# Gate products in whole units: double steps in the latent and differential attention of a hybrid layer

## Chip, cores and metric

The kernel runs on one core of one Trainium2 chip. The metric is the device time of one execution in microseconds. Three runs of the kernel before gave 2636.66, 2638.37 and 2639.43 us; their median is 2638.37.

## The reference

The whole computation is two blocks on 512 tokens of width 2048, all in fp32. The first block is two hybrid layers. A layer normalises x, multiplies by w_in (5952 columns), and feeds three attentions, of which two matter here; their outputs are gated with silu, multiplied by w_out, normalised and added to x. The second block (pooling, a diagonal state-space model, an embedding gate) is not touched.

```
C, latent ("MLA"), 4 heads:    p = softmax(causal((q_nope.k_nope + q_rope.k_rope) * 192**-0.5));  o = p @ v
A, differential, 4 heads:      p0, p1 = softmax of two 64-wide score matrices;  o = (p0 - lam * p1) @ v
B, sliding window, 16 heads:   softmax over a band of 128 keys with a sink logit
y = concat(A, B, C) * silu(concat(a_g, b_g, c_g));   out = y @ w_out
```

Both C and A run over blocks of 128 queries with a causal mask: query block qb of a head sees (qb + 1) * 128 keys. The gate columns a_g, b_g, c_g are ordinary products h @ w_in.

## The kernel before

**Products.** Every wide product takes three TensorE products in the fp32r format, each 512 columns (the tokens) long: high part by high part, high by low, low by high (lines 1923 to 1925, `product`). Weights come in units: 4 k-tiles by 256 output columns. SP loads a unit into one of four slots (ring), ScalarE casts its high part (L613, two halves), GpSimd subtracts to get the low part (L597, two halves), and TensorE then runs 2 banks x 4 k-tiles x 3 = 24 products on it. `unit` waits for wlo_done before it starts; each bank's last product raises mm_done. A ScalarE cast into a slot waits for mm_done of the unit four before. Four units with the same output columns make one round of two PSUM banks of gemm_ps, which VectorE then copies out (bank_taken).

**Attention.** An attention is 16 items, one for each head h and query block qb; item m has h = m // 4 and qb = m % 4. Each engine goes through steps m = 0 to 19 (LAST) with its own part of several items:

- TensorE (`attention`, L2132): score_step(m), then a half of a gate unit, tp_step(m - 2) (transposes of the probabilities, L2101), pv_step(m - 3) (probabilities times values, L2128).
- VectorE (L1266): copies of the gate round and the gate arithmetic at m = 9, 10, 18 and 19 (GATES_AT), out_step(m - 4) (copy of a finished head, only for qb = 3), max_step(m) (L1221, L1222), norm_step(m - 1) (L1239 to L1244).
- ScalarE (L718): the gate's tanh at m = 9 and 18, exp_step(m) (L673 or L680), pt_step(m - 2) (copy of the transposed probabilities, L700), then the weight casts (split_until) at steps that finish a unit.

A score in C is two fp32 matrices (L2082, L2083; each in two passes), in A six fp32r products of 64 rows (L2078, two row halves side by side), both followed by bf16 mask products (L2086; one in C, two in A).

**What they wait for.** C keeps its scores in s_ps, one bank for even and one for odd items: score_step(n) waits for the exponentials of item n - 2. In A the even items use both banks of s_ps, the odd ones banks 1 and 2 of to_ps (a_scores); score 1 of A also waits, at its own lines, for the rotations of A and of all copies out of av:

```
                    if m == 1:
                        pe.wait_ge(roped, l * ROPE_N + ROPES["B"])
                        pe.wait_ge(o_taken, 12 * l + 4)
                        pe.wait_ge(bank_taken[1], at[("av", l)][1] + 2)
```

av_take(1) on VectorE (L1454) raises that bank_taken[1]. tp_step(n) waits for norm_step(n) (normed) and, since there is one bank t_ps for all transposes of C and A, for pt_step(n - 1) (p_copied). pv_step(n) waits for p_copied of item n; pt_step(n) waits for tp_step(n) and pv_step(n - 2).

**Which half where.** HALF_AT maps a step to a half unit h (unit h // 2, bank h % 2). In C and A it is h + h // 6: steps 0 to 5, 7 to 12 and 14 to 17 have a half of 12 products, steps 6, 13, 18 and 19 none. ScalarE casts the weights four units ahead at the step of each odd half. C is interleaved with the gate columns "bg0", A with "cg", B with "ag"; behind C come the 576 products of "aqk" and the 192 of "av".

Of the kernel before, what the change touches and what calls it, by code (L numbers as in the profile page):

```python
# [188 lines left out]
def build_program(nc, x, positions, w_in, w_uq, w_ukv, w_out, p_2, w_in_2, w_pool_2, w_glu_2, w_out_2, w_ple_2,  # L189
                  w_ple_gate_2, params, ssm_params, consts, out):  # L190
    at, UNITS, ROUNDS = plan_units()
    with ExitStack() as ctx:
# [49 lines left out]
        c_at, n = {}, 0  # L242
# [141 lines left out]
            return l * ATT_ITEMS + FIRST[br] + m, m // 4, m % 4  # L384

        LAST = 16 + 4
        HALF_AT = {br: {h + h // 6 if br != "B" else h: h for h in range(16)} for br in "CAB"}
        GATES_AT = {br: {9: 0, 18: 1} if br != "B" else {8: 0, 16: 1} for br in "CAB"}
        ROPES = {"C": 0, "A": 3, "B": 11}
        ROPE_N = 20  # L390
# [214 lines left out]
        def _(act):  # L605
# [112 lines left out]
            def attention(l, br, key, g0):  # L718

                u0 = at[key][0]  # L720
                for m in range(LAST):
# [11 lines left out]
                    if m - 1 in GATES_AT[br] and g0 % GATE_ROUNDS < SPILLED:  # L733
                        gate_store(g0 + GATES_AT[br][m - 1])
                    if HALF_AT[br].get(m, 0) % 2 and (br != "B" or m != 15):
                        split_until(u0 + HALF_AT[br][m] // 2 + 1 + RING)
                    if m == 16 and br == "B":
# [1179 lines left out]
        def _(pe):  # L1917
# [56 lines left out]
            def one_pair(key, p, j, op=wide_op, banks=PAIR, order=(0, 1, 2, 3), ps=gemm_ps, tiles_of=None):  # L1974

                u0, r0 = at[key]
                unit(p * 4 + (u0 + j), j, [p + r0, p + r0] if ps is gemm_ps else None, banks, op,
                     order[j] * UK, UK, j == 0, j == 3, ps, VERS[tiles_of] + 4 * j if tiles_of else None)
# [61 lines left out]
            def score_step(l, br, m):  # L2040
                n, h, qb = item(l, br, m)
                q = slice(qb * 128, qb * 128 + 128)
                nk = (qb + 1) * 128
                if br == "B" and m:
                    pe.wait_ge(shifted, l * 16 + m)
                elif br == "C" and m:
                    if n >= 2:
                        pe.wait_ge(exped, n - 1)
                elif br == "A" and m:
                    pe.wait_ge(exped, n - 1)  # L2050
# [4 lines that stand above are left out]
                elif n:  # L2055
                    pe.wait_ge(exped, n)
                if br == "B":
                    w0 = 0 if qb else 128
                    g = h // 2
                    if qb == 0:  # L2060
                        pe.wait_ge(roped, l * ROPE_N + ROPES["B"] + 1 + 2 * (h + 1))
                    for a in range(2):
                        for s in range(2):
                            mm = pe.matmul(s_ps[:, a, s * 256 + w0:(s + 1) * 256],  # L2064
                                           tiles[64 * a:64 * a + 64, 4 + 2 * h + s, q],
                                           k_dup[64 * a:64 * a + 64, g, (qb - 1) * 128 + w0:nk],
                                           start=True, stop=True)
                    mm.then_inc(scores, 1)
                    return
                if br == "A":  # L2070
                    if qb == 0:
                        pe.wait_ge(qk_ready, 8 * l + 2 * (h + 1))
                    q_hi, k_hi = qk_high(h), qk_high(4 + h)
                    q_lo, k_lo = tiles_r[:, h], tiles_r[:, 4 + h]
                    for i, (left, right) in enumerate(((q_hi, k_hi), (q_hi, k_lo), (q_lo, k_hi))):
                        for c in range(2):
                            rows = slice(64 * c, 64 * c + 64)
                            pe.matmul(a_scores[n % 2][:, c, 0:nk], left[rows, q], right[rows, 0:nk],  # L2078
                                      start=i == 0, stop=i == 2, skip_group_check=True)
                else:  # L2080
                    c = n % 2
                    pe.matmul(s_ps[:, c, 0:nk], tiles[:, 12 + h, q], tiles[:, h, 0:nk], start=True, stop=False)  # L2082
                    pe.matmul(s_ps[:, c, 0:nk], tiles[:, 9 + h // 2, q], tiles[:, K_ROPE[h % 2], 0:nk],  # L2083
                              start=False, stop=True)
                for c in range(2) if br == "A" else (n % 2,):
                    mm = pe.matmul((a_scores[n % 2] if br == "A" else s_ps)[:, c, q], ident_b[:], mask_b[:],  # L2086
                                   start=False, stop=True, skip_group_check=True)
                mm.then_inc(scores, 1)

            def tp_step(l, br, m):  # L2090
                n, h, qb = item(l, br, m)
                b = n % 2
                pe.wait_ge(normed, n + 1)
                if n:
                    pe.wait_ge(p_copied, n)
                if br == "B" and m == 0:
                    pe.wait_ge(roped, (l + 1) * ROPE_N)
                blocks = [(0, k) for k in range(qb + 1)] if br != "B" else \
                    [(a, 2 * s + k) for a in range(2) for s in range(2) for k in range(0 if qb else 1, 2)]
                for a, k in blocks:  # L2100
                    mm = pe.transpose(t_ps[:, a, k * 128:(k + 1) * 128],  # L2101
                                      prob[n % 3][:, a * 512 + k * 128:a * 512 + (k + 1) * 128], ident)
                mm.then_inc(p_tp, 1)

            def pv_step(l, br, m):
                n, h, qb = item(l, br, m)
                b = n % 2
                q = slice(qb * 128, qb * 128 + 128)
                pe.wait_ge(p_copied, n + 1)
                if br == "B" and m == 0:  # L2110
                    pe.wait_ge(v_in, l + 1)
                if qb == 0 and br == "C" and h >= 2:
                    pe.wait_ge(o_taken, n // 4 - 1)
                elif qb == 0 and n // 4 and (br != "C" or h == 0):
                    pe.wait_ge(o_taken, n // 4)
                if br == "B":
                    g = h // 2
                    for s in range(2):
                        for a in range(2):
                            for k in range(0 if qb else 1, 2):  # L2120
                                mm = pe.matmul(o_ps[64 * a:64 * a + 64, s, q],
                                               v_b[:, qb - 1 + k, 64 * g:64 * g + 64],
                                               prob_t[:, b, (4 * a + 2 * s + k) * 128:(4 * a + 2 * s + k + 1) * 128],
                                               start=k == (0 if qb else 1), stop=k == 1)
                else:
                    v0 = 8 if br == "A" else 4
                    for k in range(qb + 1):
                        mm = pe.matmul(o_ps[:, 1 if br == "A" else h % 2, q], tiles[:, v0 + k, h * 128:(h + 1) * 128],  # L2128
                                       prob_t[:, b, k * 128:(k + 1) * 128], start=k == 0, stop=k == qb)
                mm.then_inc(pv_done, 1)  # L2130

            def attention(l, br, key):  # L2132

                for m in range(LAST):
                    if m < 16:
                        score_step(l, br, m)
                    if br == "B" and m == 8:
                        tp_step(l, br, m - 2)
                    if m in HALF_AT[br]:
                        p, j, f = HALF_AT[br][m] // 8, HALF_AT[br][m] // 2 % 4, HALF_AT[br][m] % 2  # L2140
                        one_pair(key, p, j, banks=[PAIR[0], None] if f == 0 else [None, PAIR[1]])
                    if br == "B" and 16 <= m < 19:
                        one_pair(("wo", l), 0, (m - 16) // 2, tiles_of=f"y{l}",
                                 banks=[PAIR[0], None] if m != 17 else [None, PAIR[1]])
                    if 2 <= m < 18 and (br != "B" or m != 8):
                        tp_step(l, br, m - 2)
                    if 3 <= m < 19:
                        pv_step(l, br, m - 3)
# [3 lines left out]
            for l in range(LAYERS):  # L2152
# [56 lines left out]
                    tokens_unit(u0 + 2 + n, 2 + n, sub_op, 2 * n, n == 0, n == 1)  # L2209
                pe.wait_ge(bank_taken[0], r0 + 4)  # L2210
                pe.wait_ge(roped, l * ROPE_N + 3)
                attention(l, "C", ("bg0", l))
                pairs(("aqk", l), 4)
                pe.wait_ge(p_copied, l * ATT_ITEMS + 16)
                pe.wait_ge(o_taken, 12 * l + 4)
                for n in range(8):
                    tokens_unit(at[("av", l)][0] + n, n % 4, wide_op, 2 * n, n == 0, n == 7)
                pe.wait_ge(bank_taken[0], at[("av", l)][1] + 2)
                attention(l, "A", ("cg", l))
                for j in range(4):  # L2220
                    one_pair(("bq0", l), 0, j)
                    if j == 2:
# [237 lines left out]
```

## Time and profile before

| what | value |
|---|---|
| runs | 2636.66, 2638.37, 2639.43 us |
| profiled execution, its own time | 2639.56 us |
| span of its records | 2637.7 us |
| TensorE busy | 2586.3 us, 98% of the span |
| VectorE, ScalarE, GpSimd busy | 53%, 36%, 45% |
| mean DMA rate | 106 GB/s |

The busy share of TensorE counts modelled ends: a product's record is longer than the distance to the next one, so records overlap. For what TensorE can do, take distances between starts. A line such as "x2" in a timeline merges neighbours of one kind.

### The profile page before, as it was taken

Reading aid. Unit: us, or ns where it says so; the run is one execution under the profiler, and the core shown is the slowest. Engines: PE = TensorE matmul, PEld = TensorE weight load, DVE = VectorE, ACT = ScalarE, POOL = GpSimd, SP = SyncE. Lnnn points to the kernel's source line nnn. Section 1 sums busy time; section 2 is a strip of 40 time slices with the busy share of each in tenths; the row PEclk is TensorE's granted clock in tenths of the full one; section 3 lists DMA queues with packets and bytes.
Section 4 is the critical chain, followed back from the end, with each engine's and each line's share of the span. In section 5 each row is a group of like instructions: output and inputs, shape, how many; then the busy total and the mean of one; then the engine's idle time right before and its main releaser. Section 6 shows DMA issues by size and latency. Waiting matters only on the chain. (4 is left out here: it accounts for less than half of the span.)

```text
span 2637.7 us, 35046 instructions
## 1 busy us (share of the span) xinstructions
PE 2586.3 (98%) x12646; PEld 2090.9 (79%) x12646; DVE 1398.2 (53%) x2141; ACT 950.1 (36%) x1926; POOL 1189.9 (45%) x864
## 2 busy tenths in 40 slices
PE   8999999999999999999999999999999999999996
PEld 6887887887888788788788788878777778888885
DVE  6553146537622855314653764286899995211533
ACT  5333224325522523322432552241555443322322
POOL 5552453442444455245345244444333456555542
PEclk9999999999999999999999999999999999999998
DMA  5342342341333334234234133343322423432331
GB/s 179 104 131 73 88 128 72 104 131 50 136 96 96 115 109 132 73 89 130 69 105 131 49 137 95 96 141 109 103 88 88 152 80 112 164 96 92 107 99 73
DMA packets 254128, 278.31 MB, mean 106 GB/s; under 512 B 22961, under 2 KB 239665, under 8 KB 251825
## 3 DMA queue, kind: packets, MB, share of 16 engines
q1 hardware_dynamic: 248144, 231.78, 29.7%
q10 hardware_dynamic: 5856, 44.80, 4.4%
q8 instruction: 84, 1.38, 0.2%
q14 instruction: 44, 0.35, 0.0%
HBM read 246.13 MB, written 20.97 MB: 101 GB/s over the span
## 5 line engine op out<-in xcount | busy, mean ns | idle before, releaser
L597 POOL TENSOR_TENSOR w_lo<-w_raw,w_hi 128x512 fp32r<-128x512 f32 x856 | 1184.7, 1407 | 1411.6 <-ACT w_hi L613 1410.8
L1923 PE MATMUL gemm_ps<-act_hi,w_hi 128*128 128x512 f32 x2624 | 1038.9, 396 | 3.0 <-ACT att L931 1.8
L1925 PE MATMUL gemm_ps<-act_hi,w_lo 128*128 128x512 f32 x2624 | 1022.6, 390 | 0.0
L1924 PE MATMUL gemm_ps<-act_lo,w_hi 128*128 128x512 f32 x2624 | 1021.8, 389 | 0.0
L613 ACT CAST w_hi<-w_raw 128x512 fp32r<-128x512 f32 x856 | 486.3, 618 | 1256.3 <-PE gemm_ps L1925 1050.3
L1923 PEld LDWEIGHTS gemm_ps<-act_hi,w_hi 128*128 128x128 f32 x2624 | 492.7, 188 | 124.7 <-issue 23.1
L1925 PEld LDWEIGHTS gemm_ps<-act_hi,w_lo 128*128 128x128 f32 x2624 | 492.6, 188 | 104.5
L1924 PEld LDWEIGHTS gemm_ps<-act_lo,w_hi 128*128 128x128 f32 x2624 | 493.1, 188 | 100.3 <-issue 2.2
L1098 DVE TENSOR_TENSOR tiles<-gemm_ps,rstd 128x512 f32<-128x512 f32 (+1 forms) x46 | 31.5, 691 | 252.6 <-PE gemm_ps L1925 252.5
L1521 DVE COPY tiles<-gemm_ps 128x512 f32 x28 | 19.4, 692 | 187.0 <-PE gemm_ps L1925 187.0
L1864 DVE TENSOR_TENSOR tiles<-gemm_ps,att 128x512 f32<-128x512 f32 x16 | 11.1, 692 | 149.4 <-PE gemm_ps L1925 149.4
L1923 PE MATMUL to_ps<-act_hi,w_hi 128*128 128x512 f32 x192 | 75.9, 395 | 0.0
L1925 PE MATMUL to_ps<-act_hi,w_lo 128*128 128x512 f32 x192 | 74.8, 389 | 0.0
L1924 PE MATMUL to_ps<-act_lo,w_hi 128*128 128x512 f32 x192 | 74.7, 389 | 0.0
L1221 DVE TENSOR_REDUCE small<-s_ps 128x1 f32<-128x128 f32 (+5 forms) x48 | 26.7, 557 | 79.9 <-PE s_ps L2086 79.5
L673 ACT ACTIVATE att<-att,small 128x256 f32<-128x256 f32 (+1 forms) x128 | 60.1, 473 | 13.4 <-DVE small L1217 13.4
L2022 PE MATMUL gemm_ps<-act_hi,w_hi 128*128 128x512 f32 x96 | 39.7, 414 | 25.3 <-ACT act_hi L873 13.1
L1895 DVE SCALAR_TENSOR_TENSOR att<-att 128x512 f32 x14 | 11.3, 809 | 89.9 <-ACT att L1067 89.9
L2101 PE MATMUL to_ps<-cst,att 128*128 128x128 f32 x384 | 57.6, 272 | 0.0
L1207 DVE CUSTOM_DVE_ANT_0 att<-s_ps,cst 128x256 f32<-128x256 f32 (+1 forms) x128 | 42.3, 385 | 28.6 <-PE s_ps L2064 28.3
L680 ACT ACTIVATE att<-s_ps,small 128x128 f32<-128x128 f32 (+1 forms) x64 | 31.8, 499 | 68.7 <-DVE small L1222 68.7
L2101 PEld LDWEIGHTS to_ps<-cst,att 128*128 128x128 f32 x384 | 46.7, 139 | 11.1 <-issue 0.5
(437 smaller groups left out, 3222.3 us busy)
## 6 DMA issues: line engine op xcount, KB each, us to landing
w_raw<-in_w_in_dram SPq DMA_DIRECT2D x248, 512.0 KB
w_raw<-in_w_out_dram SPq DMA_DIRECT2D x96, 512.0 KB
w_raw<-in_w_ple_gate_dram SPq DMA_DIRECT2D x32, 512.0 KB
att<-tiles SPq DMA_DIRECT2D x136, 64.0 KB, 2.0
gate_scratch<-att ACTq DMA_DIRECT2D x16, 512.0 KB, 2.7
att<-x_scratch ACTq DMA_DIRECT2D x2, 4096.0 KB, 12.8
w_raw<-in_w_glu_dram SPq DMA_DIRECT2D x32, 256.0 KB
tiles<-in_x_dram ACTq DMA_DIRECT2D x4, 1024.0 KB, 8.0
```

Of the source, the lines that this page charges most:

```text
L597: ins = pool.tensor_tensor(w_lo[:, s, k], w_raw[:, s, k], w_hi[:, s, k].bitcast(F32), ALU.subtract)
L613: act.copy(w_hi[:, slot, k:k + 2], w_raw[:, slot, k:k + 2]).then_inc(whi_done, 1)
L673: act.activation(v, v, ACT.Exp, bias=sm[:, 4 + j:5 + j], scale=SCALE[br], accum_out=sm[:, 8 + j:9 + j])
L680: last = act.activation(prob[n % 3][:, c * 512:c * 512 + nk], src, ACT.Exp, bias=sm[:, 4 + c:5 + c], scale=SCALE[br], accum_out=sm[:, 8 + ...
L1098: tt(dst, ps[:, f, :], scale[:], ALU.mult).then_inc(bank_taken[f], 1)
L1207: last = dve.tensor_tensor_reduce(prob[n % 3][:, 256 * j + w0:256 * j + 256], s_ps[:, j // 2, j % 2 * 256 + w0:j % 2 * 256 + 256], band[:, ...
L1221: own.link(dve.reduce_max(sm[:, 0:nc_], src, AX))
L1923: pe.matmul(ps, left_hi, right_hi, start=first, stop=False, skip_group_check=True)
L1924: pe.matmul(ps, left_hi, right_lo, start=False, stop=False, skip_group_check=True)
L1925: return pe.matmul(ps, left_lo, right_hi, start=False, stop=last, skip_group_check=True)
L2022: pe.matmul(ps, w_hi[:, slot, k, w], act_hi[:, kt], start=first, stop=False, skip_group_check=True)
L2101: mm = pe.transpose(t_ps[:, a, k * 128:(k + 1) * 128], prob[n % 3][:, a * 512 + k * 128:a * 512 + (k + 1) * 128], ident)
```

## The change

The steps of C and A are paired on TensorE. In double step `step` (m = 2 * step) it issues the scores of items m and m + 1, the transposes of item m - 2, the value products of item m - 3, then a whole unit of 24 gate products (both banks) if `step` is in UNIT_STEPS, then the transposes of m - 1 and the value products of m - 2. Double steps 4 (m = 8 and 9) and 9 have no unit. HALF_AT of C and A now lists only odd halves at steps 1, 3, 5, 7, 11, 13, 15 and 17; VectorE does not use it and ScalarE reads from it when to cast, so its casts for the unit four ahead stand at these steps (before: 1, 3, 5, 8, 10, 12, 15, 17). `attention` stays for B, whose table is unchanged.

```diff
--- before.py
+++ after.py
@@ -384,7 +384,9 @@
             return l * ATT_ITEMS + FIRST[br] + m, m // 4, m % 4
 
         LAST = 16 + 4
-        HALF_AT = {br: {h + h // 6 if br != "B" else h: h for h in range(16)} for br in "CAB"}
+        UNIT_STEPS = (0, 1, 2, 3, 5, 6, 7, 8)
+        HALF_AT = {br: {h: h for h in range(16)} if br == "B" else
+                   {2 * step + 1: 2 * u + 1 for u, step in enumerate(UNIT_STEPS)} for br in "CAB"}
         GATES_AT = {br: {9: 0, 18: 1} if br != "B" else {8: 0, 16: 1} for br in "CAB"}
         ROPES = {"C": 0, "A": 3, "B": 11}
         ROPE_N = 20
@@ -2129,6 +2131,25 @@
                                        prob_t[:, b, k * 128:(k + 1) * 128], start=k == 0, stop=k == qb)
                 mm.then_inc(pv_done, 1)
 
+            def attention_pairs(l, br, key):
+
+                for step in range(LAST // 2):
+                    m = 2 * step
+                    for n in (m, m + 1):
+                        if n < 16:
+                            score_step(l, br, n)
+                    if 2 <= m < 18:
+                        tp_step(l, br, m - 2)
+                    if 3 <= m < 19:
+                        pv_step(l, br, m - 3)
+                    if step in UNIT_STEPS:
+                        u = UNIT_STEPS.index(step)
+                        one_pair(key, u // 4, u % 4)
+                    if 2 <= m + 1 < 18:
+                        tp_step(l, br, m - 1)
+                    if 3 <= m + 1 < 19:
+                        pv_step(l, br, m - 2)
+
             def attention(l, br, key):
 
                 for m in range(LAST):
@@ -2209,14 +2230,14 @@
                     tokens_unit(u0 + 2 + n, 2 + n, sub_op, 2 * n, n == 0, n == 1)
                 pe.wait_ge(bank_taken[0], r0 + 4)
                 pe.wait_ge(roped, l * ROPE_N + 3)
-                attention(l, "C", ("bg0", l))
+                attention_pairs(l, "C", ("bg0", l))
                 pairs(("aqk", l), 4)
                 pe.wait_ge(p_copied, l * ATT_ITEMS + 16)
                 pe.wait_ge(o_taken, 12 * l + 4)
                 for n in range(8):
                     tokens_unit(at[("av", l)][0] + n, n % 4, wide_op, 2 * n, n == 0, n == 7)
                 pe.wait_ge(bank_taken[0], at[("av", l)][1] + 2)
-                attention(l, "A", ("cg", l))
+                attention_pairs(l, "A", ("cg", l))
                 for j in range(4):
                     one_pair(("bq0", l), 0, j)
                     if j == 2:
```

## Rows read from the trace of the kernel before

**Rows 1.** The page: busy time, share of the span and instructions of each engine.

```profile
PE 2586.3 (98%) x12646; PEld 2090.9 (79%) x12646; DVE 1398.2 (53%) x2141; ACT 950.1 (36%) x1926; POOL 1189.9 (45%) x864
```

**Rows 2.** Stretch table: us, PE, PEld, DVE, ACT, POOL busy, PEclk, DMA share, GB/s.

```profile
280.00:400.00 120.00, 120.00 (x531) 99.39 (x530) 32.47 (x39) 28.79 (x51) 58.98 (x44) 1.00 0.42 118
```

**Rows 3.** Timeline of PE, C of layer 0, steps 3 to 5: start, us.

```profile
215.78 0.38 PE L2101 MATMUL to_ps<-cst,att 128*128 128x128 f32 x2
...
216.67 0.22 PE L2086 MATMUL s_ps<-mask_b,ident_b 128*128 128x128 bf16 x1
...
217.01 0.39 PE L1924 MATMUL gemm_ps<-act_lo,w_hi 128*128 128x512 f32 x1
...
219.55 0.49 PE L2101 MATMUL to_ps<-cst,att 128*128 128x128 f32 x3
219.87 0.61 PE L2128 MATMUL to_ps<-att,tiles 128*128 128x128 f32 x4
220.32 0.60 PE L2082 MATMUL s_ps<-tiles 128*128 128x256 f32 x2
```

**Rows 4.** Timeline of PE, C of layer 0, steps 6 and 15 to 16.

```profile
226.46 0.22 PE L2086 MATMUL s_ps<-mask_b,ident_b 128*128 128x128 bf16 x1
226.52 0.28 PE L2101 MATMUL to_ps<-cst,att 128*128 128x128 f32 x1
...
267.78 0.39 PE L2128 MATMUL to_ps<-att,tiles 128*128 128x128 f32 x2
...
268.24 0.39 PE L1924 MATMUL gemm_ps<-act_lo,w_hi 128*128 128x512 f32 x1
```

**Rows 5.** Timeline of PE, A of layer 0, steps 4 and 5.

```profile
426.46 0.50 PE L2128 MATMUL to_ps<-att,tiles 128*128 128x128 f32 x3
426.89 0.39 PE L2078 MATMUL to_ps<-sub_lo,sub_hi 64*128 64x256 f32 x2
...
427.45 0.28 PE L2086 MATMUL to_ps<-mask_b,ident_b 128*128 128x128 bf16 x2
```

**Rows 6.** Timelines of PE and ACT at the end of C of layer 0.

```profile
275.29 1.33 PE L2128 MATMUL to_ps<-att,tiles 128*128 128x128 f32 x8
...
274.93 0.58 ACT L700 COPY att<-to_ps 128x512 f32<-128x512 f32 x1 [3.17 <-PE to_ps L2101]
```

**Rows 7.** Timelines of PE and DVE at the start of A of layer 0.

```profile
407.75 0.28 PE L2086 MATMUL s_ps<-mask_b,ident_b 128*128 128x128 bf16 x2
...
407.91 1.40 DVE L1454 TENSOR_SCALAR tiles<-to_ps,col 128x512 f32<-128x512 f32 x2
```

**Rows 8.** Timelines of PE, POOL and DVE, A, steps 4 and 8 (last row).

```profile
423.06 0.28 PE L2086 MATMUL s_ps<-mask_b,ident_b 128*128 128x128 bf16 x2
...
423.43 2.54 POOL L597 TENSOR_TENSOR w_lo<-w_raw,w_hi 128x512 fp32r<-128x512 f32 x2 [5.65 <-ACT w_hi L613]
...
423.85 0.90 DVE L1222 TENSOR_SCALAR small<-small 128x2 f32<-128x2 f32 x1
...
424.85 1.40 DVE L1240 TENSOR_SCALAR att<-att,small,col 128x512 f32<-128x512 f32 x1
426.29 0.75 DVE L1241 SCALAR_TENSOR_TENSOR att<-att,small 128x512 f32<-128x512 f32 x1
...
439.79 0.55 DVE L1240 TENSOR_SCALAR att<-att,small,col 128x512 f32<-128x512 f32 x1
```

**Rows 9.** Timelines of ACT and DVE, C of layer 0, step 4.

```profile
216.20 0.37 ACT L700 COPY att<-to_ps 128x256 f32<-128x256 f32 x1 [1.34 <-PE to_ps L2101]
...
217.51 1.24 DVE L1244 TENSOR_SCALAR att<-att,small 128x512 f32<-128x512 f32 x1
```

**Rows 10.** Timelines of DVE and ACT, A of layer 0, steps 9 and 1.

```profile
441.04 1.28 DVE L1098 TENSOR_TENSOR att<-gemm_ps,rstd 128x512 f32<-128x512 f32 x2
...
411.67 0.69 DVE L1221 TENSOR_REDUCE small<-to_ps 128x2 f32<-128x512 f32 x1 [0.98 <-PE to_ps L2086]
...
413.42 0.20 ACT L680 ACTIVATION_READ_ACCUMULATOR att<-to_ps,small 128x1 f32 x1
```

## The prediction

> **What bounds the kernel.** I read the page's engine line first: TensorE is busy 98% of the span, VectorE 53%, ScalarE 36%, GpSimd 45% [rows 1]. Nothing else comes near, so a change pays only by taking nanoseconds off TensorE's queue, and costs wherever that queue waits. The table by stretches gives the price of a gate product: 120.00 us hold 531 products of 512 columns at the full granted clock, about 0.227 us from start to start (some records may be missing; the pairs of rows below give 0.23 too) [rows 2]. Then I read TensorE's timeline inside an attention, because the change reorders nothing else.
>
> **What a piece costs.** From start to start, an fp32 pass of 128 columns takes 0.11 us: three transposes 0.32, four passes of probabilities times values (two matrices in two passes each) 0.45 [rows 3]. A bf16 mask product takes 0.06 [rows 4]. From a mask product to the second gate product behind it is 0.34; less the mask (0.06) and one gate product (0.227) that leaves 0.06 of bubble [rows 3]. From two value passes to the second gate product is 0.46; less 0.22 and 0.227 that leaves 0.01 [rows 4]. So **a gate run costs 0.06 to enter behind a mask, 0.01 behind an fp32 pass**. Between its second product (217.01) and the first transpose behind its twelfth (219.55) lie 2.54 us, for 11 steps of 0.227, 2.50: restarting a run costs another 0.04 [rows 3].
>
> **What the change gains.** Per attention C or A, 16 runs of 12 become 8 runs of 24. Before, 14 enter behind a mask and 2 behind value passes: 14 x 0.06 + 2 x 0.01 = 0.86. After, the first enters behind a mask, the second behind a transpose, six behind value passes: 0.06 + 7 x 0.01 = 0.13. Saved 0.73. Eight restarts fewer, 0.035 taken for each (an estimate a little under the 0.04; bounds 0 and 0.05): 0.28. Together 1.0 per attention, **4.0 us for the four**. That is also nearly the ceiling: 8 bubbles and the work itself stay. The new pair mask then score is not in the trace for A; a score there is 64 rows high, and entering it from three value passes costs 0.43 instead of 0.34 [rows 5]. I take the same 0.09, so nothing changes; bounds 0 and 0.18, that is -0.7 to +0.7 per A.
> No instruction is added or removed on any queue. VectorE and ScalarE keep their order item by item; ScalarE's casts for the unit four ahead follow the whole unit (odd m, as now or a step earlier), with a ring of four units in front; SP's loads and GpSimd's low parts follow by semaphores. I cost these at nothing: the cover is three whole units of 24 x 0.227 = 5.4 us, and without it a unit would wait for a cast and a subtraction.
> The Trainium skill, in "TensorE: Matmul & The Clock Gate", section "Step-by-step: what each phase is for", says that the next tile's weights load while this tile's product runs. Taken literally, entering a run would be free and the gain 0 instead of 4.0; the 0.06 behind a mask disagrees, and the rows decide.
>
> **What the change costs.** Each half unit was 2.7 us of cover between a score and what waits for it. Four places lose it. The price of a wait: the last copy of an attention ends at 275.51 (274.93 + 0.58), value passes were ready to go on at 275.40, yet the eight passes from 275.29 take 1.33 instead of 1.06. So the hole is 0.27: 0.11 until the copy ends, and **0.16 of release and restart on top** [rows 6].
>
> (a) Score 1 of A. It writes banks 1 and 2 of to_ps, so it waits until VectorE has scaled the last two token tiles of av (L1454), which ends at 407.91 + 1.40 = 409.31. Now half 0 stands ahead of it. After, it is ready behind score 0's two masks: 407.75 + 0.12 + 0.09 = 407.96 [rows 7]. Late by 1.35, plus 0.16: **1.5 us**, in both layers. What sets L1454's time is the last av unit, which does not move.
>
> (b) Transpose 7, in the double step m = 8 and 9, which has no unit. Norm 7 stands on VectorE behind max 8, thus behind score 8. The same surroundings exist now at m = 4 of A (unit end, copy of 256 columns, two casts, score with one block): mask at 423.06, GpSimd starts its two subtractions at 423.43, VectorE's small L1222 takes 0.90, L1240 1.40 where the same shape takes 0.55 undisturbed, L1241 0.75, and that ends at 427.04, 3.98 behind the mask [rows 8]. After, TensorE has between mask 8 and transpose 7: masks 0.12, entry 0.09, score 9 0.56 [rows 5], masks 0.12, three transposes 0.33, four passes 0.45: 1.67. Wait 3.98 - 1.67 + 0.16 = **2.5 us in A**. In C the norm ends at 217.51 + 1.24 = 218.75, 2.08 behind mask 4 [rows 9]; TensorE needs 0.06 + 0.9 + 0.06 + 0.33 + 0.45 = 1.8. Wait 0.28 + 0.16, say **0.5 us in C**.
> Here a rule bears on the row. The Trainium skill ("SBUF — State Buffer", section "Who interferes with whom") says that VectorE in a two-port mode, or with two inputs from SBUF, and GpSimd lock a shared port pair for a whole instruction. The trace agrees: L1222, on two columns, ends at 424.75, where the first of two subtractions of 1.27 ends (424.70), and L1240 lies across the second (to 425.97). Without such a lock (b) would be about 1.8 shorter in each A.
>
> (c) Score 11 of A needs exp 9. Behind norm 7 VectorE has the two gate copies of m = 9 (1.28), then max 9, and from a max of this size to the end of its exponentials are 413.62 - 411.67 = 1.95 [rows 10]. On the clock of mask 8: 3.98 + 1.28 + 1.95 = 7.21. TensorE, restarted at 4.14, runs transposes 0.44, six passes 0.67, entry 0.09, score 10 about 0.7 (0.56 for 256 columns, more for 384), masks 0.12, entry 0.09: 6.25. Wait 0.96 + 0.16 = **1.1 us in A**. In C the same sum puts exp 9 level with score 11 (maxima and exponentials are half as wide): 0. Next in line are score 13 and transpose 10: a unit of 5.5 us stands in front, and I find over 1 us of slack.
>
> (d) Transpose 14, m = 16, where no score stands ahead any more. It waits until item 13's 256 columns are copied out of the one bank t_ps. In C's template transposes 215.78, two value passes, ready at 216.22, copy ends at 216.20 + 0.37 = 216.57 [rows 3, 9]: 0.35 + 0.16 = **0.5 us, four times**.
>
> **Sum.** A: 1.5 + 2.5 + 1.1 + 0.5 = 5.6, twice 11.2. C: 0.5 + 0.5 = 1.0, twice 2.0. Less 4.0: **+9.2 us**. TensorE is full to the end, so nothing gives it back. The profiled execution took 2639.56 us (span 2637.7, 1.9 around it): 2648.8. The median shown, 2638.37, lies 1.2 below it, so I predict 2647.6.
>
> **Rivals.**
> 1. Not slower: GpSimd misses VectorE in (b). Place: L1222 and L1240 behind score 8. It decides if GpSimd's first subtraction starts later than 0.8 us behind the mask (0.37 in the rows), or both have ended before. Then L1222 saves nearly all of its 0.90 (0.75), L1240 0.85, L1241 about 0.2: 1.8 per A, and in C 0.3 until the copy of item 6 is next late; (c) shifts along. 9.2 - 4.2 = +5.0, 2643.4, within 0.2%. For: the trace has untouched norms too. Against: the casts that release GpSimd hang on the unit's end, as does score 8. 0.17.
> 2. Joining gains nothing: the bubbles belong to the start of any run or reappear between mask and score. +13.2, 2651.6. For: mask then score is unseen. Against: the 0.01 behind value passes. By the page on TensorE named above the gain is 0 as well. 0.06.
> 3. The waits of (b) and (c) push further down (score 13, transposes 9 and 10 late by 1 us in each A): +11.2, 2649.6. 0.12.
> 4. Faster: the waits are all covered and only the 4.0 remains: 2634.4. (a) and (d) are waits by construction, so 0.02.
> 5. The change does not do what it says, the waits of the old order remaining as before: the diff moves every gate product of C and A, so 0.
> The forecast, all four places within their bounds: 0.63.
>
> **Range.** Bounds: (a) 1.3 to 1.7, (b) in A 0.7 to 2.9, (c) 0.5 to 1.9, (d) 0.4 to 0.6, gain 3.0 to 4.4 less the 0.7 of the unseen pair. The low end takes in rival 1, the high end rival 3 and half of 2: 2642.2 to 2651.2. A measurement of this kernel can tell about 0.2%, 5.3 us, from no change. Slower by more: forecast, rivals 2 and 3, most of it, 0.78; within: rival 1, rival 4 and the forecast's low tail, 0.21; faster 0.01, since even all gain and no wait is 0.15%.
>
> **What would show it.** TensorE's granted clock stays 1.00 in both attentions. In the timeline, gate runs of 24, masks mostly followed by fp32 passes; each C about as long as before, each A 4 to 5 us longer. Holes: before the second L2078 group of A behind L1454, before L2101 behind L1241 (A) or L1244 (C) at m = 9, before L2078 behind ScalarE's L680 at m = 11, before the first L2101 at m = 16 behind L700. The forecast is wrong if the hole at m = 9 of A is under 1 us, if there is none behind L1454, or if the B attention or the long streams change.

## The result, and the profile after

| kernel | median of all runs, us | runs | profiled execution, us | its span, us |
|---|---|---|---|---|
| before | 2638.37 (2636.66 to 2639.43) | 5 | 2639.56 | 2637.7 |
| changed | 2651.35 (2648.02 to 2652.68) | 5 | 2651.35 | 2649.6 |

The changed kernel is slower by 13.0 us, a ratio of 1.0049 with a 95% interval of 1.0038 to 1.0059. The direction was as predicted; the forecast was +9.2 us, and the median lies 0.15 us above the end of the range. In the runs below one execution of the kernel with filler (6729.98 us) and one of the kernel before beside it (10684.78 us) stand far apart and are not in the ratios. Line numbers of the changed kernel and of the kernels made from it are two higher than before (scores of A L2080, masks L2088, transposes L2103, values L2130, gate products L1925 to L1927).

The page's engine line of the changed kernel answers to [rows 1]:

```profile
PE 2589.5 (98%) x12646; PEld 2094.9 (79%) x12646; DVE 1403.8 (53%) x2141; ACT 949.2 (36%) x1926; POOL 1188.2 (45%) x864
```

It shows nearly nothing: the same 12646 products, and 98% as before. The table by stretches shows more if its stretches are the four attentions, each from its first score to the first product behind its last value passes. Columns: from and to in us, length, PE busy (instructions), granted clock, DMA share, GB/s. The kernel before, layer 0 (layer 1 has 76.58 and 72.43 at a clock of 1.00 too):

```profile
199.88:276.48 76.60, 76.59 (x393) 1.00 0.23 68
407.27:479.70 72.43, 72.42 (x441) 1.00 0.24 67
```

The same view of the changed kernel:

```profile
198.85:275.78 76.93, 76.38 (x394) 1.00 0.23 68
406.56:485.27 78.71, 74.80 (x442) 0.96 0.21 62
1061.37:1138.36 76.99, 76.44 (x394) 1.00 0.23 68
1269.14:1348.04 78.90, 74.99 (x442) 0.96 0.22 62
```

The two C attentions are longer by 0.33 and 0.41 us, the two A by 6.28 and 6.47. Together 13.5 us; the spans differ by 11.9, the remaining -1.6 lying in stretches that the change does not touch (1.0 of it before the first attention), as much as executions of one kernel differ among themselves. So everything is inside the four attentions, as the forecast had it, and two things are new. TensorE's idle time in an A is now 3.9 us (78.71 less 74.80), where it was 0. And **the granted clock is 0.96 in A, not 1.00**. The same view in steps of 2 us finds where:

```profile
408.00:410.00 2.00, 1.25 (x9) 0.75 0.00 1
410.00:412.00 2.00, 2.00 (x6) 0.50 0.24 46
446.00:448.00 2.00, 1.04 (x5) 0.64 0.40 78
1272.00:1274.00 2.00, 2.00 (x8) 0.65 0.16 23
1310.00:1312.00 2.00, 2.00 (x11) 0.53 0.71 236
```

Four times, twice in each A, the clock falls to 0.50 (1.2 instead of 2.4 GHz) and comes back a few microseconds later. A value between, such as 0.75, is a stretch that has both levels in it: of the stretch from 408 to 410, the first microsecond has 1.00 and the second 0.51. The Trainium skill, "TensorE: Matmul & The Clock Gate", section "What's actually happening", lists the same two levels in its table of states. TensorE's timeline at the start of A of layer 0 shows what came before the first fall (in brackets the idle time and its releaser):

```profile
407.04 0.28 PE L2088 MATMUL s_ps<-mask_b,ident_b 128*128 128x128 bf16 x2
408.75 0.39 PE L2080 MATMUL to_ps<-sub_lo,sub_hi 64*128 64x256 f32 x2 [1.42 <-DVE tiles L1456]
...
411.50 0.63 PE L1926 MATMUL gemm_ps<-act_lo,w_hi 128*128 128x512 f32 x1
411.93 0.63 PE L1927 MATMUL gemm_ps<-act_hi,w_lo 128*128 128x512 f32 x1
412.35 0.43 PE L1925 MATMUL gemm_ps<-act_hi,w_hi 128*128 128x512 f32 x1
```

From mask 0 to score 1 are 1.71 us where the step takes 0.21 (0.12 for the masks and 0.09 to enter): a hole of 1.5, released by VectorE's L1456, as step (a) said. Then the gate products start 0.43 apart instead of 0.227 [rows 2], until 412.35. The kernel before has such places too, outside the attentions. Two stand behind a much longer idle time of 6.54 us, at 869.95 and 1726.12; the first is shown. A third stands behind 1.59 us at its very end, where hardly any products follow. But an idle time of 1.60 us among long products brings no fall (last row): the granted clock is 1.00 from 2150 to 2170.

```profile
869.95 0.76 PE L2022 MATMUL gemm_ps<-act_hi,w_hi 128*128 128x512 f32 x1 [6.54 <-ACT act_hi L873]
...
870.00:872.00 2.00, 2.00 (x5) 0.50 0.17 58
...
2161.72 0.47 PE L1923 MATMUL to_ps<-sub_hi,w_hi 128*128 128x512 f32 x1 [1.60 <-issue]
```

The second place in A is m = 8 and 9, timelines of PE, DVE and POOL; they answer to [rows 8]:

```profile
442.97 0.28 PE L2088 MATMUL s_ps<-mask_b,ident_b 128*128 128x128 bf16 x2
...
444.19 0.61 PE L2130 MATMUL to_ps<-att,tiles 128*128 128x128 f32 x4
446.96 1.11 PE L2103 MATMUL to_ps<-cst,att 128*128 128x128 f32 x4 [2.16 <-DVE att L1243]
447.87 1.49 PE L2130 MATMUL to_ps<-att,tiles 128*128 128x128 f32 x6
...
443.75 0.89 DVE L1224 TENSOR_SCALAR small<-small 128x2 f32<-128x2 f32 x1
444.74 1.38 DVE L1242 TENSOR_SCALAR att<-att,small,col 128x512 f32<-128x512 f32 x1
446.15 0.75 DVE L1243 SCALAR_TENSOR_TENSOR att<-att,small 128x512 f32<-128x512 f32 x1
...
443.34 2.50 POOL L599 TENSOR_TENSOR w_lo<-w_raw,w_hi 128x512 fp32r<-128x512 f32 x2 [6.70 <-ACT w_hi L615]
```

This is the template of [rows 8] nearly number for number: GpSimd starts 0.37 behind mask 8, the small L1224 takes 0.89, L1242 1.38, and L1243 ends 3.93 behind the mask (3.98 forecast). From the value passes to transpose 7 are 2.77 us where such passes need 0.45: a hole of 2.3. Behind it four transposes take 0.91 (447.87 less 446.96) instead of 0.44 and six value passes 1.42 instead of 0.76, at the lower clock. Score 11 then starts 0.21 behind its mask (0.33 in layer 1): the hole of step (c) is as good as absent.

Step (d), m = 16 of A:

```profile
476.09 0.39 PE L2130 MATMUL to_ps<-att,tiles 128*128 128x128 f32 x2
476.80 0.52 PE L2103 MATMUL to_ps<-cst,att 128*128 128x128 f32 x3 [0.33 <-ACT att L702]
```

0.71 for two value passes of 0.22: 0.5, as forecast. In C, at m = 9 and in the pairs of scores:

```profile
234.51 0.65 PE L2084 MATMUL s_ps<-tiles 128*128 128x256 f32 x2
235.43 0.22 PE L2088 MATMUL s_ps<-mask_b,ident_b 128*128 128x128 bf16 x1
...
235.82 0.61 PE L2130 MATMUL to_ps<-att,tiles 128*128 128x128 f32 x4
236.64 0.63 PE L2103 MATMUL to_ps<-cst,att 128*128 128x128 f32 x4 [0.21 <-DVE att L1246]
```

The hole is 0.82 less 0.45, 0.37 (forecast 0.44, taken as 0.5). A score of 256 columns straight behind a mask lasts 0.92 from its start to its mask. The kernel before, where such a score stands behind value passes:

```profile
236.62 0.60 PE L2082 MATMUL s_ps<-tiles 128*128 128x256 f32 x2
237.49 0.22 PE L2086 MATMUL s_ps<-mask_b,ident_b 128*128 128x128 bf16 x1
```

0.87: the pair of mask and score, which the forecast took as free, costs 0.05 in C, eight times in each.

### The profile page after: what moved, and what is told of

Same layout as the page of the kernel before. It is cut to its first block and busy times, and to the rows that moved or that the text cites. A ratio compares the mean times of both kernels' runs of the same rounds, so it can differ in the third digit from the quotient of the medians.

```text
span 2649.6 us, 35038 instructions
## 1 busy us (share of the span) xinstructions
PE 2589.5 (98%) x12646; PEld 2094.9 (79%) x12646; DVE 1403.8 (53%) x2141; ACT 949.2 (36%) x1926; POOL 1188.2 (45%) x864
## 3 DMA queue, kind: packets, MB, share of 16 engines
q8 instruction: 84, 1.38, 0.2%
## 5 line engine op out<-in xcount | busy, mean ns | idle before, releaser
L1925 PE MATMUL gemm_ps<-act_hi,w_hi 128*128 128x512 f32 x2624 | 1036.8, 395 | 3.0 <-ACT att L933 1.8
L1927 PE MATMUL gemm_ps<-act_hi,w_lo 128*128 128x512 f32 x2624 | 1023.4, 390 | 0.0
L1925 PEld LDWEIGHTS gemm_ps<-act_hi,w_hi 128*128 128x128 f32 x2624 | 493.5, 188 | 121.3 <-issue 20.2
L1927 PEld LDWEIGHTS gemm_ps<-act_hi,w_lo 128*128 128x128 f32 x2624 | 493.2, 188 | 104.1
L1925 PE MATMUL to_ps<-act_hi,w_hi 128*128 128x512 f32 x192 | 75.9, 395 | 0.0
L1927 PE MATMUL to_ps<-act_hi,w_lo 128*128 128x512 f32 x192 | 74.8, 389 | 0.0
L2103 PE MATMUL to_ps<-cst,att 128*128 128x128 f32 x384 | 58.5, 275 | 6.1 <-DVE att L1243 4.3
L2103 PEld LDWEIGHTS to_ps<-cst,att 128*128 128x128 f32 x384 | 45.8, 140 | 18.6 <-DVE att L1243 5.7
L702 ACT COPY att<-to_ps 128x128 f32<-128x128 f32 (+1 forms) x64 | 27.2, 426 | 88.7 <-PE to_ps L2103 88.6
```

Of the source, the lines that this page charges most:

```text
L702: act.copy(prob_t[:, b, 0:nk], t_ps[:, 0, 0:nk]).then_inc(p_copied, 1)
L1925: pe.matmul(ps, left_hi, right_hi, start=first, stop=False, skip_group_check=True)
L1927: return pe.matmul(ps, left_lo, right_hi, start=False, stop=last, skip_group_check=True)
L2103: mm = pe.transpose(t_ps[:, a, k * 128:(k + 1) * 128], prob[n % 3][:, a * 512 + k * 128:a * 512 + (k + 1) * 128], ident)
```

## The experiments

The theory after the result: the holes (a), (b) and (d) are as forecast; holes (a) and (b) each also bring the clock down, which costs some 1.5 us each time and hides (c). Its rivals: the slower stretches come from something else than the holes (the joined unit, the execution as a whole), or the sizes agree by chance. All lengths of attentions below are read as in the tables above.

**One hole alone in the old order.** Score 1 of A ahead of half 0, in the kernel before:

```diff
-                    if m < 16:
+                    if m < 16 and (br, m) != ("A", 1):
                         score_step(l, br, m)
+                    if br == "A" and m == 0:
+                        score_step(l, br, 1)
```

> The kernel before, with one edit: score 1 of A issued right behind score 0, ahead of the first half unit. Theory (a hole on TensorE costs itself and then a fall of the granted clock): a hole of 1.5 us behind L1454 in each A, then gate products at half pace that cost about 1.5 more; twice 3.0, so about 6 us slower than before, some 2644.5. Rival (a hole costs only itself): twice 1.5, some 2641.4, and gate products at 0.227 us right behind the hole.

Measured: 2642.52 us (2640.72 to 2643.39) against 2638.81, ratio 1.0014 (1.0005 to 1.0023). The two C as before; the two A, and the starts of both score 1:

```profile
406.29:481.69 75.40, 73.98 (x442) 0.98 0.23 65
1265.13:1338.93 73.80, 72.38 (x441) 1.00 0.23 66
...
408.47 0.39 PE L2078 MATMUL to_ps<-sub_lo,sub_hi 64*128 64x256 f32 x2 [1.42 <-DVE tiles L1454]
...
1267.31 0.39 PE L2078 MATMUL to_ps<-sub_lo,sub_hi 64*128 64x256 f32 x2 [1.42 <-DVE tiles L1454]
```

Two holes of the same 1.42 us; the A with a fall of the clock is 2.97 us longer than before, the one without 1.37. So a hole of this size costs 1.4, and the fall, **when it comes**, another 1.6. It does not come each time, which is why the median lies between the two expectations. A fall needs no joined unit: this kernel has none.

**The hole moved.** The changed kernel with score 1 of A behind unit 0:

```diff
-                        if n < 16:
+                        if n < 16 and (br, n) != ("A", 1):
                             score_step(l, br, n)
...
                         one_pair(key, u // 4, u % 4)
+                    if br == "A" and step == 0:
+                        score_step(l, br, 1)
```

> The changed kernel, with one edit: score 1 of A issued behind the whole first unit, which covers its wait. Theory: both the hole (1.5) and the slow products behind it (1.5) go in each A, 6 us faster than the changed kernel's 2651.35, some 2645; the granted clock still falls at m = 9 of A. Rival (holes cost only themselves): 3 us faster, some 2648.3. If a hole only moves on (score 3, transpose 0 wait instead): no gain.

Measured: 2648.99 us (2647.01 to 2649.35), ratio 1.0037 (1.0024 to 1.0051); 10.2 us over the kernel before beside it, where the changed kernel has 13.0. The hole behind L1456 is gone, and score 3, now close behind score 1, waits instead:

```profile
416.12 0.50 PE L2080 MATMUL to_ps<-sub_lo,sub_hi 64*128 64x512 f32 x2 [1.10 <-ACT att L682]
...
406.99:485.80 78.81, 74.85 (x441) 0.96 0.22 62
1269.67:1346.02 76.35, 71.98 (x441) 1.00 0.23 64
```

The hole of 1.1 brought no fall in either layer. The first A has one fall, behind (b). In the second A no fall came at all, and it is 2.5 us shorter than the first, though TensorE idles as long in it (4.4 against 4.0): the clock, not the idle time, makes that difference. Taking one thing out of a wait's way is not enough if its neighbour then stands too near.

**More work in the hole.** The changed kernel with six useless products between score 0 and score 1 of A; their results are thrown away:

```diff
+                        if (br, n) == ("A", 1):
+                            for k in range(6):
+                                pe.matmul(gemm_ps[:, k % 2, :], act_hi[:, k, 0:128], act_hi[:, k], start=True,
+                                          stop=True, skip_group_check=True)
                         if n < 16:
                             score_step(l, br, n)
```

> The changed kernel, with six useless products of 512 columns (1.4 us of work, into gemm_ps, overwritten by the unit) put between score 0 and score 1 of A. Theory: score 1 starts as late as before, but TensorE was busy, so the granted clock does not fall there and the first unit runs at 0.227 a product: 1.5 us less per A, some 2648.3, faster although work was added. Rival (the slow first unit comes from something else, as weights or banks that come late): 2651.4 or a little more.

Measured: 2648.38 us, the median of all six executions (2647.90 for the five that lie between 2647.54 and 2649.81), ratio 1.0037 (1.0023 to 1.0050). **TensorE does more, and the kernel comes out 3.0 us faster than the changed one**, from median to median; but the two ratios to the kernel before have intervals that overlap (1.0038 to 1.0059 for the changed kernel), so the times alone do not settle it. The profile says more. The filler, the stretches behind it, and the later waits of the second A:

```profile
406.85 1.65 PE L2141 MATMUL gemm_ps<-act_hi 128*128 128x512 f32 x6
...
408.00:410.00 2.00, 2.00 (x15) 1.00 0.00 0
...
406.27:483.58 77.31, 74.82 (x448) 0.98 0.22 63
1267.70:1344.33 76.63, 73.36 (x448) 1.00 0.22 64
...
1306.57 0.66 PE L2103 MATMUL to_ps<-cst,att 128*128 128x128 f32 x4 [2.15 <-DVE att L1243]
1309.62 0.50 PE L2080 MATMUL to_ps<-sub_lo,sub_hi 64*128 64x512 f32 x2 [0.78 <-ACT att L682]
```

Score 1 starts as late as in the changed kernel (1.71 behind mask 0), but no fall follows it. In the second A none follows the hole of (b) either, and there **score 11 waits for exp 9**, 0.78 us: step (c) exists, and in the changed kernel it was hidden because TensorE came there late at the lower clock. This A is the changed kernel's without any fall: 1.5 (filler for hole), 2.3, 0.8 and 0.5, less the gain of 1.0, make 4.1; measured is 76.63 less 72.44, 4.19. In the first A the clock falls behind (b), and (c) is nearly hidden (0.33 from mask to score 11): it is 0.68 longer, so that fall cost about 0.7 + 0.8 = 1.5.

**The lock by itself.** The changed kernel with the casts of the unit at m = 7 moved to m = 9, so that GpSimd's subtractions for it no longer lie beside norm 7:

```diff
-                   {2 * step + 1: 2 * u + 1 for u, step in enumerate(UNIT_STEPS)} for br in "CAB"}
+                   {2 * step + 1 + 2 * (u == 3): 2 * u + 1 for u, step in enumerate(UNIT_STEPS)} for br in "CAB"}
```

> The changed kernel, with the casts of the weights four units ahead moved from ScalarE's step m = 7 to m = 9 in C and A, so that GpSimd's two subtractions no longer lie beside norm 7. Theory (most of the wait at m = 9 is VectorE behind GpSimd): the hole before transpose 7 shrinks from 2.3 us to about 0.7 in A and from 0.37 to 0.1 or 0.2 in C, the clock does not fall there, and score 11 waits about 0.8 instead; 1.6 + 1.4 - 0.8 = 2.2 less per A, some 2646.5. Rival (VectorE's chain is long by itself): the hole keeps over 1.5 us and the time stays within 1 us of 2651.

Measured: 2645.76 us (2644.16 to 2647.39) against 2637.56, ratio 1.0031 (1.0020 to 1.0043). Norm 7 of A in layer 0 and what follows it:

```profile
441.71 0.17 DVE L1224 TENSOR_SCALAR small<-small 128x2 f32<-128x2 f32 x1
...
441.99 0.55 DVE L1242 TENSOR_SCALAR att<-att,small,col 128x512 f32<-128x512 f32 x1
...
443.37 0.66 PE L2103 MATMUL to_ps<-cst,att 128*128 128x128 f32 x4 [0.61 <-DVE att L1243]
...
446.42 0.50 PE L2080 MATMUL to_ps<-sub_lo,sub_hi 64*128 64x512 f32 x2 [0.78 <-ACT att L682]
...
406.07:481.44 75.37, 72.02 (x441) 1.00 0.23 64
1264.85:1341.78 76.93, 73.60 (x441) 0.98 0.23 63
```

L1224 takes 0.17 instead of 0.89, L1242 0.55 instead of 1.38, and the idle time ahead of transpose 7 falls from 2.16 to 0.61: the 1.6 is the collision with GpSimd, which the prediction had put at 1.8. The small hole brings no fall, in either layer, and score 11 shows its wait. The fall in the second A stands behind the hole of (a), which is unchanged here; the first A has the same hole and no fall. In C nothing came of it (76.92 and 76.98, as in the changed kernel): its hole of 0.37 is not made by GpSimd.

**Both repairs.** The two edits above together.

> The changed kernel with both repairs: six useless products between score 0 and score 1 of A, and the casts of the unit at m = 7 moved to m = 9. Theory (the clock falls in A were brought on by the two long holes, 1.5 us ahead of score 1 and 2.3 us ahead of transpose 7): the first is filled, the second is 0.8 us, so TensorE's granted clock is 1.00 through both A attentions. Each A is then the 75.37 us of the A without a fall in the run with late casts, the 1.4 to 1.6 us of products standing in the 1.5 us hole: 75.3 to 75.6. Median about 2644.4 on the runs of before at 2637.5 to 2638.5, 1.4 below the late casts alone. Rival (falls come wherever TensorE has any holes, as a matter of chance): one fall in four attentions or so as in the run with late casts, A at 76.9 in one layer, median 2645.8 or more. C as in the changed kernel, 76.9 to 77.0.

Measured: 2644.84 us (2643.23 to 2645.99) against 2638.13, ratio 1.0025 (1.0015 to 1.0034). The two A:

```profile
407.55:482.90 75.35, 73.42 (x447) 1.00 0.23 64
1267.03:1342.43 75.40, 73.46 (x447) 1.00 0.23 64
```

No fall in either, and both have the length expected. The executions spread over 2.8 us, those of the kernel before over 2.5, those of the changed kernel over 4.7. Counting the profiled executions, one of each kernel:

| idle time of TensorE | cases | falls of the clock behind it |
|---|---|---|
| 2.15 or 2.16 us, place (b) of A | 6 | 4 |
| 1.42 us, place (a) of A | 6 | 4 |
| place (a) filled | 4 | 0 |
| 0.60 or 0.61 us, place (b) with late casts | 4 | 0 |
| 1.10 us or less, all other places of C and A, also in the kernels below | all | 0 |
| 1.60 to 1.63 us, outside the attentions, among long products, every kernel | 12 | 0 |

**The repair in earnest.** Score 1 of A between the halves of unit 0; the unit at m = 7 split over m = 7 and 9, so that the double step of m = 8 and 9 has cover; casts and gate copies moved with it:

```diff
-        GATES_AT = {br: {9: 0, 18: 1} if br != "B" else {8: 0, 16: 1} for br in "CAB"}
+        GATES_AT = {br: {10: 0, 18: 1} if br != "B" else {8: 0, 16: 1} for br in "CAB"}
...
-                    if step in UNIT_STEPS:
+                    if br == "A" and step == 0:
+                        one_pair(key, 0, 0, banks=[PAIR[0], None])
+                        score_step(l, br, 1)
+                        one_pair(key, 0, 0, banks=[None, PAIR[1]])
+                    elif step == 3:
+                        one_pair(key, 0, 3, banks=[PAIR[0], None])
+                    elif step == 4:
+                        one_pair(key, 0, 3, banks=[None, PAIR[1]])
+                    elif step in UNIT_STEPS:
```

> The changed kernel with its double steps, but: score 1 of A between the halves of unit 0; the second half of unit 3 in double step 4; gate copies of the first round at m = 10; the casts of unit 3's slot at m = 9. Theory: the holes before score 1, transpose 7 and score 11 are gone, and with them every fall of the clock inside C and A; only the hole at m = 16 (0.5) stays. A about 72.1 us, C about 76.6, together 0.6 below before: some 2638, 13 us under the changed kernel. Rival (double steps are slower in themselves, or the holes move on as with score 1 behind the whole unit): over 2643.

Measured: 2639.38 us (2638.68 to 2640.40) against 2637.56, ratio 1.0006 (0.9997 to 1.0015): 11 of the 13 us are gone, and no clock falls in C or A. C is 76.60 and 76.64, as before; A 73.31 and 73.26, 0.9 above the kernel before, and 1.2 above what was expected. The rest of A's gain goes into new waits of two odd scores for ScalarE, this one and one of 0.45 at score 13 (and 0.5 at m = 16, as always):

```profile
438.70 0.39 PE L2080 MATMUL to_ps<-sub_lo,sub_hi 64*128 64x256 f32 x2 [0.63 <-ACT att L682]
```

In A, two scores issued side by side cost more in waits for the engines behind them than the 1.0 us that joining gains.

**The gain without joining.** In the kernel before, every half unit of C and A behind the value passes of its step instead of behind the mask:

```diff
                         tp_step(l, br, m - 2)
+                    if br != "B" and 2 <= m < 18:
+                        tp_step(l, br, m - 2)
+                    if br != "B" and 3 <= m < 18:
+                        pv_step(l, br, m - 3)
                     if m in HALF_AT[br]:
...
-                    if 2 <= m < 18 and (br != "B" or m != 8):
+                    if br == "B" and 2 <= m < 18 and m != 8:
...
-                    if 3 <= m < 19:
+                    if 3 <= m < 19 and (br == "B" or m == 18):
```

> The kernel before in its single steps, with each half of a gate unit in C and A moved behind the step's transposes and value products instead of between score and transposes. No double steps. Theory (what joining gained is mostly the entry behind fp32 passes, 0.05 less than behind a mask, 13 or 14 times per attention): 0.7 us less per attention, 3 in all, some 2635.4, with no hole over 0.3 us except at the end of each attention. Rival (the gain comes from runs of 24): none of it, 2638.4; or transposes behind a bare score wait and make it slower.

Measured: 2641.63 us (2641.23 to 2642.22) against 2638.81, ratio 1.0011 (1.0002 to 1.0020). C is 75.74 and 75.73, 0.86 shorter, and TensorE has no idle time in it. The edit moves 12 of the 14 halves that stood behind a mask (those of m = 0 and 1 have no transposes yet and stay), so each saves 0.07, where the bubbles of the prediction (0.06 less 0.01) had 0.05. A is 75.07 and 75.04, 2.6 longer:

```profile
433.61 0.44 PE L2101 MATMUL to_ps<-cst,att 128*128 128x128 f32 x2 [0.97 <-DVE att L1241]
...
463.85 0.33 PE L2101 MATMUL to_ps<-cst,att 128*128 128x128 f32 x1 [0.99 <-DVE att L1241]
```

Between them lie two of 0.25 and 0.22 behind copies (L1257, L700). Where a norm or a copy is late, the half unit was its cover. No clock falls behind these 0.97 and 0.99.

**Only where nothing is late.** The same in C alone (first), in C and in A except m = 7, 12 and 14 (second), and except m = 7, 8, 12 and 14 (third); for the condition `br != "B"` above stands in the third (and its opposite for `br == "B"`)

```diff
-                    if br != "B" and 2 <= m < 18:
+                    if (br == "C" or br == "A" and m not in (7, 8, 12, 14)) and 2 <= m < 18:
                         tp_step(l, br, m - 2)
```

> The kernel before, halves behind the value products in C alone. Theory: C takes 75.74 us instead of 76.6 as in the kernel with this edit in C and A, with no hole; A as before: 1.7 us faster than before, some 2637. Rival (a measurement cannot tell): the profile still shows 75.7.

> As the one before, and also in A except at m = 7, 12 and 14, the steps whose transposes waited 1.1, 0.4 and 1.2 us on norms when this edit was in all of A. Theory: A takes 0.5 to 0.7 us less than before (ten entries at 0.05), no hole over 0.3; 2.8 us faster than before in all, some 2636. Rival: VectorE's chain in A has no slack at other steps either, and holes of over 0.4 come back: slower than the one before.

> The kernel before with each half unit behind the value passes in C, and in A except at m = 7, 8, 12 and 14, where it stays between score and transposes as cover. Theory (each half moved away from a mask saves 0.05 us, and only those four places of A lack slack): C 75.74, A 72.0, no hole over 0.3 us in A, total 2.5 us below the kernel before. Rival (VectorE's lateness moves on, so another place of A shows the next hole, as m = 8 did when 7, 12 and 14 were kept): A 72.4 or more, total 1.7 below or less. Both lie within what the measurement can tell from no change; the phase durations decide.

Measured, with the lengths of C and A in us:

| kernel | median, us | before beside it | ratio (95%) | C | A |
|---|---|---|---|---|---|
| C alone | 2636.44 | 2637.56 | 0.9995 (0.9986 to 1.0004) | 75.74, 75.73 | 72.39, 72.39 |
| except 7, 12, 14 | 2637.47 | 2637.56 | 0.9999 (0.9990 to 1.0008) | 75.75, 75.73 | 72.98, 72.97 |
| except 7, 8, 12, 14 | 2636.10 | 2638.13 | 0.9993 (0.9984 to 1.0002) | 75.74, 75.73 | 72.04, 72.05 |

In the second one m = 8 of A had become late in its turn, as its rival expected: its transposes wait 0.79 us for ScalarE's copy (L700). With that half kept too, no next one appeared: A is 0.4 shorter than before, the sum over the four attentions 2.5, as the theory had it. This is the best version found. By its median it is 2.0 us below the kernel before, and its 11 executions (2635.59 to 2636.77) all lie below the 20 of that (2636.80 to 2639.25); but the interval of the ratio still holds 1, and 0.08% is less than the 0.2% that the prediction took as what a measurement can tell, so faster is shown by the lengths of the attentions only.

## Why the prediction was right and wrong

- **What bounds the kernel**: right. Nothing outside the attentions changed beyond what executions differ by.
- **The gain, 1.0 per attention**: right as a sum, read as a remainder. In C the holes 0.37 and 0.5 and 0.4 for the pairs, less the measured +0.33 and +0.41, leave 0.94 and 0.86. That a run enters for less behind an fp32 pass is shown by the 0.86 of the halves behind the value passes. At 0.07 for each of 12 halves there, the 13 entries that joining takes away from masks would make 0.9 by themselves, so how much of the gain is due to the eight restarts (0.28 in the prediction) is not shown. Their 0.04 was worked out with steps of 0.227; in that same run of 12 the ten steps from 217.01 to 219.31 take 0.230 each, so most of it lies inside the run and not at its end. In a run of 24 of the changed kernel, the 22 steps from 217.56 to 222.57 take 0.228 each. Entering a run was not free, a gain of 0 did not come, and rival 2 falls with it.
- **The pair of mask and score**: in A right (0.21 or 0.22 from mask to score where nothing waits, 0.12 for the masks and 0.09 or 0.10 to enter). In C the step "so nothing changes" failed by 0.05 in each of eight pairs: +0.8 us in all. The bounds of 0 and 0.18 had been set for A alone.
- **(a) 1.5**: right, 1.5. **(d) 0.5**: right, four times.
- **(b) 2.5 in A**: 2.3, and 0.37 in C for 0.5. The mechanism, norm 7 behind GpSimd's subtractions, was right, shown by moving the casts. Rival 1 did not come.
- **(c) 1.1 in A**: 0.8 where the clock stayed up, and 0 or 0.1 where it fell behind (b), since TensorE then came later at score 11. (In the kernel with score 1 behind unit 0 it still waited 0.37 in such a case.) **Rival 3** did not come in the changed kernel. It did in part with the late casts, where the hole of (b) was small: score 13 then started 0.50 behind its mask instead of 0.22.
- **The step that failed** is the sentence "TensorE's granted clock stays 1.00 in both attentions". The sum (a) to (d) less the gain, at full clock, is 4.1 to 4.2 per A, against 4.6 forecast. The clock fell twice in each A, about 1.5 us each, 3.0 per A, with (c) hidden by the later of them: 1.5 + 2.3 + 0.5 + 3.0 - 1.0 = 6.3, and 6.28 and 6.47 were measured. In the trace of before, the clock falls behind idle times of 6.54 us and at the very end, stays up behind one of 1.60 us among long products, and no A has a hole over a microsecond. So nothing in it showed what holes of 1.5 and 2.3 us would do among the short passes of A; the forecast took the better answer for granted and gave the other neither a term nor a bound. With it as a rival, worth 3.0 less a hidden (c) in each A, the range would have reached beyond the result.
- **Luck**: without any fall the sum would have come out, at 2 x 4.2 in A and 0.33 + 0.41 in C, 9.1 us for 9.2 forecast. That is closer than its terms were: (b) in A and (c) were too large by 0.2 and 0.3, and the 0.8 for the pairs in C was missing.

What is shown and what is not: in A, 8 of 12 holes of 1.4 us and more were followed by a fall, and none of the eight that were filled or shrunk to 0.6 (in the kernel with both repairs, all four). So, as far as these cases go, the holes are needed for the falls there. They are not enough: 4 of the 12 brought none, and neither did the idle time of 1.60 to 1.63 us outside the attentions in any of the twelve kernels, though it is longer than hole (a). It stands among products of 512 columns on 128 rows, (a) and (b) among scores of 64 rows and passes of 128 columns. Whether these neighbours matter, and what decides between the two outcomes of one and the same hole, stays open; no run here was made for either.

## What to carry to other kernels

On a TensorE that is busy throughout, count a reordering by the edges between kinds of product: here 0.05 to 0.07 us for a long run that starts behind a bf16 mask instead of an fp32 pass, which can be had by issuing the run a few instructions later. Before pieces of cover are joined, list what each one covered; here the lost covers, with the falls of the clock that they brought, cost 7.3 us in each A against 1.0 gained, while leaving the halves where a norm or a copy is late and moving only the others took 0.4 off each A. And price a long hole in a busy TensorE twice: its length, and with some chance the time behind it at half the clock; where the trace shows such a fall, useless products in the hole are worth a try.

## What the hardware showed that was not expected

- In the A attentions an idle time of 1.42 us was followed by a fall of the granted clock to 0.5 in four of six cases, one of 2.16 us in four of six, and the shorter ones (up to 1.10 us) in none. Outside them, one of 1.60 to 1.63 us among long products was followed by none in twelve cases. A fall behind (a) cost 1.6 us (75.40 less 73.80).
- With six products without use (1.65 us of TensorE) in hole (a), the clock did not fall there in four cases, and the kernel's median was 3.0 us lower, with intervals that overlap.
- In C an fp32 score straight behind a bf16 mask costs 0.05 us more than behind an fp32 pass (0.92 against 0.87 to its mask), about what a gate run does.
- The lock between VectorE and GpSimd, told in the prediction from the Trainium skill ("SBUF — State Buffer", "Who interferes with whom"), is borne out by removing the neighbour: 0.89 to 0.17 and 1.38 to 0.55 for the same two instructions.
